# Output projection's last three weight tiles run bank by bank, with the transposes of the residual sum among them

## The reference

```python
x = x + jnp.einsum('bse,ed->bsd', y, w_out[l])       # "wout": 1024 x 1024
h = rms_norm(x, norm_mlp[l])
u = jnp.square(jax.nn.relu(jnp.einsum('bsd,df->bsf', h, w_ff1[l])))   # 1024 -> 4096
x = x + jnp.einsum('bsf,fd->bsd', u, w_ff2[l])       # 4096 -> 1024
...
mod = jnp.einsum('bd,de->be', silu_c, w_ada[l]) + b_ada[l]   # second block, needs c alone
```

## Time and profile before

| | us |
|---|---|
| median of 3 runs | 1416.97 (1416.82 to 1417.31) |
| the profiled execution | 1417.1 |
| its span on the core | 1415.3 |
| PE busy | 1369.9 (97%) |
| POOL, DVE, ACT busy | 1056.2, 755.6, 710.1 |
| mean granted PE clock | 0.987 |

### The profile page before, as it was taken

How to read it: one execution, slowest core, us unless ns; L and a number is a source line. 1 busy time by engine, 2 the same in 40 slices (tenths; PEclk the granted TensorE clock), 3 DMA queues, 4 the chain that set the end, 5 groups by cost and what they waited for, 6 DMA issues and landing times.

```text
span 1415.3 us, 28941 instructions
## 1 busy us (share of the span) xinstructions
PE 1369.9 (97%) x9762; PEld 1219.6 (86%) x9762; DVE 755.6 (53%) x1616; ACT 710.1 (50%) x1129; POOL 1056.2 (75%) x469
## 2 busy tenths in 40 slices
PE   6998999999999998899999999999999999999997
PEld 6887899998877886899999999999977777788886
DVE  4655433334258526349991176666688888611113
ACT  6444555555345443435556543343355555556664
POOL 6554688886678885668888877777777777788885
PEclk9999999998999999999999999999999999999999
DMA  8443677774545456535555554444444445475552
GB/s 305 154 164 107 243 289 279 274 264 146 198 147 180 149 172 259 199 134 179 179 187 183 178 165 162 157 155 162 157 155 163 163 165 169 156 259 193 193 191 98
DMA packets 72651, 263.02 MB, mean 186 GB/s; under 512 B 8208, under 2 KB 9104, under 8 KB 72224
## 3 DMA queue, kind: packets, MB, share of 16 engines
q1 hardware_dynamic: 72608, 262.46, 53.6%
HBM read 259.81 MB, written 2.62 MB: 185 GB/s over the span
## 4 chain that ended last, share of the span: by engine, by line
PE 89%; DVE 5%; issue 2%; ACT 1%; POOL 1%; DMA 1%; SPq 0%; POOLq 0%; ACTq 0%; DVEq 0%
PE bank L849 14%; PE bank L867 14%; PE bank L850 14%; PE bank L851 14%; PE bank L868 13%; PE bank L869 13%; PE bank L1242 3%; DVE arena L1718 1%; DMA raw<-stream 1%; PE bank L965 1%; POOL wlo L431 1%; PE bank L1224 1%; PE bank L923 0%; DVE bank L1346 0%; PE bank L1154 0%
## 5 line engine op out<-in xcount | busy, mean ns | idle before, releaser
L431 POOL TENSOR_TENSOR wlo<-raw,whi 128x1024 fp32r<-128x1024 f32 x432 | 1041.8, 2423 | 315.5 <-ACT whi L493 312.4
L493 ACT ACTIVATE whi<-raw 128x1024 fp32r<-128x1024 f32 x432 | 455.7, 1057 | 350.9 <-PE bank L869 255.3
L849 PE MATMUL bank<-xh,whi 128*128 128x256 f32 x1600 | 462.2, 289 | 6.9 <-DVE xl L1314 4.5
L850 PE MATMUL bank<-xl,whi 128*128 128x256 f32 x1600 | 455.3, 285 | 0.0
L851 PE MATMUL bank<-xh,wlo 128*128 128x256 f32 x1600 | 455.0, 284 | 0.0
L867 PE MATMUL bank<-whi,xh 128*128 128x512 f32 x800 | 321.2, 402 | 9.7 <-DVE xl L1549 2.5
L849 PEld LDWEIGHTS bank<-xh,whi 128*128 128x128 f32 x1600 | 309.8, 194 | 12.0 <-POOL wlo L431 6.5
L868 PE MATMUL bank<-wlo,xh 128*128 128x512 f32 x800 | 313.2, 392 | 0.0
L869 PE MATMUL bank<-whi,xl 128*128 128x512 f32 x800 | 313.0, 391 | 0.0
L850 PEld LDWEIGHTS bank<-xl,whi 128*128 128x128 f32 x1600 | 310.0, 194 | 1.2
L851 PEld LDWEIGHTS bank<-xh,wlo 128*128 128x128 f32 x1600 | 309.5, 193 | 0.0
(11 more groups left out here) (279 smaller groups left out, 1155.5 us busy)
## 6 DMA issues: line engine op xcount, KB each, us to landing
raw<-stream SPq DMA_DIRECT2D x432, 512.0 KB, 3.3
arena<-ada SPq DMA_DIRECT2D x48, 512.0 KB, 4.8
arena<-rows SPq DMA_DIRECT2D x5, 512.0 KB, 8.6
xs<-x SPq DMA_DIRECT2D x2, 512.0 KB, 4.6
arena<-rows SPq DMA_DIRECT2D x1, 1024.0 KB, 5.4
x_spill<-xs SPq DMA_DIRECT2D x1, 1024.0 KB, 6.2
xs<-x_spill SPq DMA_DIRECT2D x1, 1024.0 KB, 6.0
out<-arena SPq DMA_DIRECT2D x2, 512.0 KB, 2.6
```

The costliest lines, as they stand in the source:

```text
L431: nc.gpsimd.tensor_tensor(wlo[:, slot, :], raw[:, slot, :], whi[:, slot, :].bitcast(F32), ALU.subtract).then_inc(lo_done, 1)
L493: nc.scalar.activation(whi[:, slot, :], raw[:, slot, :], ACT.Copy).then_inc(hi_done, 1)
L849: nc.tensor.matmul(dst, h_, xh[:, k, :], start=(k == 0), stop=False)
L850: nc.tensor.matmul(dst, h_, xl[:, k, :], start=False, stop=False)
```

## The change

The last three tiles of "wout" (k = 5, 6, 7) are no longer run one after the other over all banks. For each bank in turn the three tiles' nine matmuls are run, so bank 0 is complete after a quarter of that work; a tile counts as used with its part for bank 3. Between these, PE makes 12 of the 16 transposes of the sum: those of positions 0 to 127 ahead of banks 2 and 3, and half of the others ahead of bank 3's last three matmuls. The transposes go to banks 4, 5, 0, 1 (`T_BANKS`). The last four stand between the first and second halves of the first two f_tiles (`first_two`). ACT and DVE read the banks in that order, and ACT rounds the second of the ring's tiles ahead of the transposes' results, the third and fourth behind them. Only eight, not twelve, column matmuls stay ahead of the feed-forward part; four move behind it. Nine, not twelve, modulation tiles are made before it (`ADA_IN_FFN = 9`), and SP's loads of them move accordingly.

```diff
-ADA_IN_FFN = 12
+ADA_IN_FFN = 9
...
             for n in range(T_FFN, T_FFN + 10):
                 tile(n % R, n * P, n - R + 1)
-                if n < T_FFN + 2:
-                    ada_tile(n - T_FFN + 2 * R + 2)
-                elif n % 2 == 0:
-                    ada_tile((n - T_FFN) // 2 - 1 + ADA_IN_FFN)
+                if n % 2 == 0:
+                    ada_tile((n - T_FFN) // 2 + 2 * R + 2)
...
+            def upper_among(group, gains):
+                for b in range(4):
+                    act.wait_ge(acc_ready, acc_filled(group, b))
+                    for j in range(2):
+                        k = 2 * b + j
+                        last = nc.scalar.activation(xh[:, k, :], bank[T_BANKS[b]][:, j * T:(j + 1) * T], ACT.Copy,
+                                                    scale=gains[:, k:k + 1])
+                    last.then_inc(S("turned_hi"), 1)
...
-            his(T_WOUT + R + 2, T_FFN + R)
-            upper("mlp_T", c_("mlp"))
+            upper_of(T_WOUT + R + 2, T_FFN + 2)
+            upper_among("mlp_T", c_("mlp"))
+            upper_of(T_FFN + 2, T_FFN + R)
...
+            def first_two(base, turned, between):
+                for ks in (range(KC // 2), range(KC // 2, KC)):
+                    for n in (base, base + 1):
+                        f_tile(n % R, n + 1, bank[4 + n % 2][:, 0:T], turned, ks)
+                    if ks[0] == 0:
+                        between()
...
+                for b in range(4):
+                    for k in range(KC - late, KC):
+                        if turned and b == 0 and k % 2 == 0:
+                            pe.wait_ge(S("turned_lo"), turn(turned, 4, k // 2 + 1))
+                        ahead(b, k)
+                        tile(k, banks=(b,), used=b == 3)
+
+            def turn_of(group, src, ready, tt, bs):
+                for b in bs:
+                    pe.wait_ge(S(ready), 2 * tt + b // 2 + 1)
...
+                    if tt:
+                        last.then_inc(acc_ready, 1)
...
+            def x1_turn(b, k):
+                at = (b, k - KC)
+                if at in ((2, -3), (3, -3)):
+                    turn_of("mlp_T", xres, "x1_done", 0, (0, 1) if b == 2 else (2, 3))
+                if at == (3, -1):
+                    turn_of("mlp_T", xres, "x1_done", 1, (0, 1))
+
+            m_group_by_banks(T_WOUT, "wout", 3, "y", before=late_heads, within={3: att_turn}, ahead=x1_turn)
...
-            ada_columns(2)
-            transposes("mlp_T", "mlp", xres)
...
-            for g in range(3, 8):
+            for g in range(2, 8):
                 ada_columns(g)
...
-                if 2 <= i < 2 + ADA_FIRST - ADA_IN_FFN:
-                    ada_tile(ADA_IN_FFN + i - 2)
+                if i < ADA_FIRST - ADA_IN_FFN:
+                    ada_tile(ADA_IN_FFN + i)
```

More of the change, by code:

```diff
@@ L65, in acc_freed @@
         return "xg_out", bank + 1
+    if group == "mlp_T":
+        return (("turned_lo", turn("y", 4, 3)), ("turned_lo", turn("y", 4, 4)), ("x1_done", 1), ("x1_done", 2))[bank]
+    if group == "ffn":
+        return (("turned_lo", turn("mlp", 4, 3)), ("turned_lo", turn("mlp", 4, 4)), ("x1_done", 3), ("x1_done", 4))[bank]
     if group == "merged_T":
@@ L359, in _ @@
                 tile(n % R, n * P, n - R + 1)
-                if n < T_FFN + 2:
-                    ada_tile(n - T_FFN + 2 * R + 2)
-                elif n % 2 == 0:
-                    ada_tile((n - T_FFN) // 2 - 1 + ADA_IN_FFN)
-            first = ADA_IN_FFN + R + 26
+                if n % 2 == 0:
+                    ada_tile((n - T_FFN) // 2 + 2 * R + 2)
+            first = T_FFN + 10
             with sp.Fori(0, 6) as i:
@@ L368, in _ @@
                         tile(n % R, i * (2 * R * P) + n * P, i * (2 * R) + (n - R + 1))
-                    n = ADA_IN_FFN + R + u
+                    n = 2 * R + 7 + u
                     ada_tile(n, i * (R * P) + n * P, i * R + (n - R + 1))
+            ada_tile(ADA_FIRST - 1)
             for n in range(first + 48, T_IN2_F + 8):
@@ L840, in _, with f_tile @@
         def _(pe):
-            def f_tile(slot, count, dst, turned=None):
+            def f_tile(slot, count, dst, turned=None, ks=range(KC)):
                 pe.wait_ge(lo_done, count)
-                for k in range(KC):
+                for k in ks:
                     if turned and k % 2 == 0:
@@ L851, in f_tile @@
                     last = nc.tensor.matmul(dst, l_, xh[:, k, :], start=False, stop=(k == KC - 1))
-                last.then_inc(tile_used, 1)
+                if KC - 1 in ks:
+                    last.then_inc(tile_used, 1)
+            def first_two(base, turned, between):
[4 more added lines that the diff above has]
+                        between()
             def m_tile(slot, count, ah, al, group=None, start=False, final=False, banks=range(4),
@@ L891, in m_group, with m_group_by_banks, tile @@
                         part()
+            def m_group_by_banks(a, group, late, turned=None, before=lambda k: None, within={}, ahead=lambda b, k: None):
+                def tile(k, **kw):
+                    m_tile((a + k) % R, a + k + 1, xh[:, k, :], xl[:, k, :], final=(k == KC - 1), **kw)
+                for k in range(KC - late):
+                    before(k)
+                    if turned and k % 2 == 0:
+                        pe.wait_ge(S("turned_lo"), turn(turned, 4, k // 2 + 1))
+                    kw = dict(group=group if k == 0 else None)
+                    if k in within:
+                        tile(k, banks=(0, 1), used=False, **kw)
+                        within[k]()
+                        tile(k, banks=(2, 3), **kw)
+                    else:
+                        tile(k, **kw)
+                for b in range(4):
+                    for k in range(KC - late, KC):
+                        if turned and b == 0 and k % 2 == 0:
+                            pe.wait_ge(S("turned_lo"), turn(turned, 4, k // 2 + 1))
+                        ahead(b, k)
[3 more added lines that the diff above has]
+                    pe.wait_ge(S(ready), 2 * tt + b // 2 + 1)
+                    if tt == 0:
+                        name, n = acc_freed(group, b)
+                        pe.wait_ge(S(name), n)
+                    for j in range(2):
+                        k = 2 * b + j
+                        last = nc.tensor.transpose(bank[T_BANKS[b]][:, j * T + tt * P:j * T + (tt + 1) * P],
+                                                   src[:, tt, k * P:(k + 1) * P], ident[:, :])
+                    if tt:
+                        last.then_inc(acc_ready, 1)
             def m_group_by_halves(a, group, twice, turned=None, before_last=lambda: None):
@@ L912, in transposes @@
                 for tt in tts:
[L913 to L916, removed]
+                    pe.wait_ge(S("unturned"), scaled_at(name, tt + 1))
                     for b in range(4):
@@ L978, in ada_columns @@
             def ada_columns(g):
+                if g == 0:
+                    pe.wait_ge(S("ones_set"), 1)
                 pe.wait_ge(ada_used, 4 * (g + 1))
@@ L1122, in m_of @@
                     m_tile(slot, count_, uh[:, u, :], ul[:, u, :], **kw)
-                f_tile(base % R, base + 1, bank[4][:, 0:T], name_of_turn)
-                f_tile((base + 1) % R, base + 2, bank[5][:, 0:T])
+                first_two(base, name_of_turn, lambda: turn_of("mlp_T", xres, "x1_done", 1, (2, 3)))
                 m_of((base + 2) % R, base + 3, 0, 1, group=group)
@@ L1327, in turned_shifted, with turned_among @@
                 turned(name, None)
+            def turned_among(name, gains):
+                for b in range(4):
+                    v.wait_ge(S("turned_hi"), turn(name, 4, b + 1))
+                    for j in range(2):
+                        k = 2 * b + j
+                        last = stt(xl[:, k, :], bank[T_BANKS[b]][:, j * T:(j + 1) * T], gains[:, k:k + 1],
+                                   xh[:, k, :].bitcast(F32), ALU.mult, ALU.subtract)
+                    last.then_inc(S("turned_lo"), 1)
             def ada_tile(n):
```

5 lines of the change are left out of this document (2 added, 3 removed).

## The result

The changed kernel takes 1420.09 us (median of 22 runs, 1415.12 to 1421.76) against 1417.15 for the kernel before on the same chips; the ratio is 1.0018 with a 95% interval of 1.0011 to 1.0025. So it is 2.9 us slower by the medians and 2.6 us by the ratio (1.6 to 3.5 us by the interval). The profiled execution took 1420.54 with a span of 1418.7.

The account below looks back on a forecast made before the run. PE, busy for 97% of the span and holding 89% of the chain, was taken as the bound. 1417.1 + 1.0 (ACT) + 1.2 (behind the feed-forward part) gave 1419.3, predicted as 1419.2, range 1416.3 to 1421.6.

Parts of the forecast that it names:

- no change: About 0.2%, 2.8 us: what a measurement of this kernel was said to be able to tell from no change.
- PE up to the f_tiles: Output projection to f_tiles: no transpose waits for its sum, "wout" ends at 152.0, and the first f_tile starts about 154.0.
- ACT becomes the bound: Ahead of the first m_tile: scalings, roundings and sums of squares delay ACT's first unit, so the m_tile starts 1.0 us later.
- Behind the feed-forward part: Eight extra column instructions at the lower clock cost 2.0 us, 0.8 hidden by slack: +1.2 us, between +0.1 and +2.4.
- The sum: Whole kernel: 1417.1 + 1.0 + 1.2 = 1419.3, with 1419.2 predicted as the median.
- what follows ACT's queue: From ACT's sums of squares to the first m_tile: unit at 163.3, m_tile at 165.1, PE idle about 2.7 us before it.
- the prediction's own last line: Wrong if the first m_tile starts before 163 or after 166.5, or if the clock is low there.
- the low stretch at 457.66: Rival later in the program: this 3.41 us low-clock window may go, giving 1417.6 us; chance 0.20.
- the clock's rival: Rival: the clock falls under the first f_tiles, up to 2.2 us lost, time 1421.2; chance 0.22.
- The rule on transposes: At the f_tiles: if transposes do not count as matmul work, a clock drop is likelier, with time 1421.2.

Follow-up runs that it names:

- e1: Changed kernel with ACT's roundings of the ring's third and fourth tile moved between the second and third scaling; 1414.74 us, ratio 0.9991.
- e5: Changed kernel with the last four transposes ahead of the f_tiles, which run whole; 1415.29 us, ratio 0.9987.
- e4: Kernel before with nine modulation tiles ahead of the feed-forward part and group 2's columns behind it, no interleaving; 1412.82 us, ratio 0.9975.
- e2: Changed kernel with group 2's four columns moved to just ahead of the feed-forward part's last m_tile; 1419.95 us, ratio 1.0027.
- e11: Changed kernel with the last four transposes ahead of the f_tiles and one rounding in ACT's idle between the scalings; 1413.40 us, ratio 0.9981.
- e3: Changed kernel with, behind the feed-forward part, the row behind the transposes and DVE's scaling ahead of the addition; 1419.83 us, ratio 1.0018.
- e8: Kernel before with only the row behind the transposes and DVE's scaling ahead of the addition, behind the feed-forward part; 1416.58 us, ratio 1.0001.

## Why the prediction was right, and where it was not

The forecast was 1419.2, 2.2 us slower and inside the 2.8 us that I had set as no change. The measurement is 1420.09, inside the range and 2.9 us slower. The direction was right, and the size nearly. But the interval of the ratio, 1.0011 to 1.0025, leaves out 1: with 22 runs a change of 0.2% can be told from none. And the number came out partly by luck: errors in both directions cancelled, as follows.

*PE up to the f_tiles.* Right in all but tenths. None of the interleaved transposes waited; each set of four took 0.36 us (144.96 to the next matmul at 145.32), not 0.5, and the last matmul of "wout" ended 0.2 us earlier than worked out. The first f_tile was due at 154.0 and came at 152.26 + 1.37 = 153.6.

*ACT becomes the bound.* The order of ACT is the cause, as foretold: e1 and e5 each took it away in another manner and moved the m_tile by 2.8 and 3.0 us. The sizes agree as well, +1.0 predicted and +1.06, +1.00 and +1.04 in three profiles, idles of 1.8 and 2.7 us predicted and 1.71 and 3.04 measured. But the +1.0 is made of two terms that are wrong by about the same. The unit was due at 163.3 and started at 161.05 + 1.37 = 162.4, 0.9 us early, since the scalings, roundings and sums each began or ran a little earlier than priced. From there to the m_tile 1.8 us were priced, and 2.62 were measured, 0.8 more: the hold of DVE's small operation by POOL's product. I had POOL's product ending at 162.5 and did not ask what else it would hold up. ACT's queue alone would have given an estimated +0.1.

*Behind the feed-forward part.* +1.2 predicted, +1.59 in the profile, with the release moved from POOL to PE as foretold. The size is not a constant, though. It was near 0 where the clock fell late (e1, e4), 0.38 in e2 and 1.2 in e11. I had priced it from one profile. The price of 0.25 us for an instruction at the lower clock was too high: from start to start they cost 0.21 in both kernels. But the clock fell 2.8 us after the first of them and not 3.4 as before, so about 21 of 48 were slow and not 8 of 40. The Trainium skill ("TensorE: Matmul & The Clock Gate", LDWEIGHTS) gives a weight load as its columns over 1.2, 107 ns for 128, with no term for the clock. That agrees with the spacing at full clock, 48 instructions in 5.4 us in e4, and not with the 0.21 us at the lower one.

*The sum left a term out.* The step that failed is the one on what follows ACT's queue: I worked out an idle of 2.7 us ahead of the first m_tile and priced only the idle. The clock fell 1.1 us behind its end and cost about 1.6 us more, in the changed kernel's profile; in e2's it cost about 2.8 and in e3's nothing. By the prediction's own last line, that it is wrong if the clock is low there, this part is wrong. The profile ends 4.77 us above the kernel before, starts taken out, against 2.2 forecast: 1.70 behind the first m_tile, 0.4 behind the feed-forward part, and 0.4 left between the low stretch at 457.66 that was gone and the one at 1031 that came. I had foreseen neither of these two in the sum, and that they nearly cancel is luck again. My own rows had the hint: an idle of 2.04 us stood ahead of the fall at 457.66, the fourth window of the earlier trace rows and the row. I had put the clock's rival beneath the f_tiles instead, at a chance of 0.22; there the clock was full from 151 to 163 us in all ten profiles of kernels with nine modulation tiles ahead, the changed one among them. Had the rival stood at the m_tile, the forecast would have been 1419.2 + 1.6 = 1420.8 for the runs in which it falls; half of the 22 times are at 1420.4 to 1421.8.

*The rule on transposes.* The Trainium skill's sentence that a transpose does not count as matmul work for the clock ("TensorE: Matmul & The Clock Gate", Part 4) would have made a fall beneath the f_tiles likelier. There was none, neither in the changed kernel nor in e4, where 3.7 us of columns and transposes alone and 1.28 us of idle passed at 1.00. In the kernel before and in e8, though, the clock did fall while PE made transposes, at 153.4 to 154.0 and at about 152.9. So these runs neither bear the sentence out nor refute it.

*What I priced far too low* was what the part `ADA_IN_FFN = 9` could give: I costed it at DVE's freedom and 0.9 us. Alone it was worth about 3 us: the first m_tile came 2.87 earlier, 1.09 at the f_tile and 1.78 within the two f_tiles, which took 7.73 us in the kernel before and 5.95 in e4. The 1.78 are the clock (21 matmuls in 4.45 us, at 0.21 against 0.12). e8, which keeps the 24 column instructions, still has a mean clock of 0.72 from 151 to 163 us, as the kernel before; the ten profiles with 16 have 1.00. That 0.9 us less of column work is what ended the fall fits all twelve, but it was not varied alone: the nine modulation tiles and DVE's earlier freedom came with it each time.

Left open: what decides in which executions the clock falls after an idle of 2 to 3 us. In e3 3.04 us passed without a fall, in the changed kernel and in e2 they did not; the idle of about 2.05 us that the kernel before has ahead of 457 us was followed by a fall in five of the twelve profiles and by none in seven. That the times spread because of these two cases is my reading of three profiles; no profile was taken of each time. Nor was DVE's hold taken away alone, for instance by moving the small operation behind `ul`.

## What to carry to other kernels

When work is interleaved to start an engine earlier, write out the queue of the engine that feeds it, and move what no longer has a cover into that engine's own idle: here two roundings of 1 us, 5.8 us later than in e1, cost the whole gain. Follow what they move as well: the products of POOL came late with them and held up an operation of DVE on two columns. Count an idle of TensorE like the ones here, 2.0 to 3.0 us, twice, once for itself and once for the lower clock that followed it in some executions, and judge a change at such a place by the median of many runs. A sum that comes out right should be compared term by term, since two of its terms here were wrong and cancelled. And measure the parts of a change alone: the smallest part here was the good one.

## What the runs showed of the hardware that was not expected

An operation of DVE on 128x2 took 0.17 us with POOL idle and up to 1.80 with a product of POOL under way, and then ended 0.01 to 0.03 us behind that product, in seven profiles of seven. One-column matmuls and transposes for 3.7 us, and 1.28 us of idle behind them, left the clock full (e4), while in the kernel before it fell about 3.5 us after the first of 24 column instructions, with PE busy all the time. One of the 48 column instructions took 0.11 us at the full clock (e4) and 0.21 at the lower (changed kernel). The same idle, in the same place of the same code, was followed by a low stretch of 3.4 us in one execution and by none in another, and the times of the changed kernel spread over 6.6 us.
